# Storing an expert gate table in four 512 KB parts with 1 KB runs, and loading it back for eight expert blocks at a time

## The reference

```python
s1 = jnp.einsum('thd,kd->thk', q[:, :, 0], sub_k1)      # 8 heads, 128 keys on each side
s2 = jnp.einsum('thd,kd->thk', q[:, :, 1], sub_k2)
v1, i1 = lax.top_k(s1, 16); v2, i2 = lax.top_k(s2, 16)
cand = v1[..., :, None] + v2[..., None, :]
top, pos = lax.top_k(cand, 16)                          # 16 experts for each head and token
gate = jax.nn.softmax(top, axis=-1)
act = jax.nn.gelu(jnp.einsum('thkd,td->thk', u_tab[eidx], xb))
return jnp.einsum('thk,thkd->td', gate * act, v_tab[eidx])
```

## Time and profile before

| | us |
|---|---|
| median of 3 runs | 2424.49 |
| the runs | 2418.18, 2424.49, 2425.27 |
| the profiled execution, its own time | 2419.71 |
| its span (first to last instruction) | 2417.7 |
| TensorE busy | 2244.0 (93% of the span) |
| VectorE busy | 1726.0 (71%) |
| ScalarE busy | 909.4 (38%) |
| mean DMA rate over the span | 253 GB/s |

### The profile page before, as it was taken

How to read it: one execution, slowest core, us unless ns; L and a number is a source line. 1 busy time by engine, 2 the same in 40 slices (tenths; PEclk the granted TensorE clock), 3 DMA queues, 4 the chain that set the end, 5 groups by cost and what they waited for, 6 DMA issues and landing times.

```text
span 2417.7 us, 41224 instructions
## 1 busy us (share of the span) xinstructions
PE 2244.0 (93%) x16262; PEld 2080.3 (86%) x16262; DVE 1726.0 (71%) x3078; ACT 909.4 (38%) x1568; POOL 895.3 (37%) x1063
## 2 busy tenths in 40 slices
PE   6999987989899989899999899999998999999997
PEld 3877766877669988888999899999998999999997
DVE  4646586435735445568799887777876789999988
ACT  3333342220122111222344676666763333333333
POOL 3310310110304555336321044544444346565561
PEclk9988998998979999999999999999999999999999
DMA  5530740122818999858676489989999999999994
GB/s 154 178 94 18 241 130 20 56 84 71 280 72 255 303 293 308 249 164 300 196 246 210 156 281 350 334 316 348 324 342 378 388 376 397 405 404 403 403 405 184
DMA packets 328799, 611.62 MB, mean 253 GB/s; under 512 B 27712, under 2 KB 216144, under 8 KB 327584
## 3 DMA queue, kind: packets, MB, share of 16 engines
q0 software_dynamic: 90240, 316.05, 36.4%
q1 hardware_dynamic: 219936, 267.78, 33.1%
q10 hardware_dynamic: 18432, 25.17, 2.8%
HBM read 484.45 MB, written 124.45 MB: 252 GB/s over the span
## 4 chain that ended last, share of the span: by engine, by line
PE 57%; DVE 21%; DMA 15%; ACT 3%; issue 2%; POOL 2%; ACTq 0%; DVEq 0%; SPq 0%; POOLq 0%
PE PS L1197 56%; DMA RAW<-in_uT 8%; DMA u_rows<-arena 4%; DVE LO L2371 3%; DVE arena L1810 3%; DVE GU L2551 2%; DVE OH L2538 2%; POOL u_rows L605 2%; DVE arena L1849 1%; DVE arena L1819 1%; ACT HI L1060 1%; DVE arena L2066 1%; DVE arena L1816 1%; DVE BR L1849 0%; DVE rstd L1867 0%
## 5 line engine op out<-in xcount | busy, mean ns | idle before, releaser
L1060 ACT ACTIVATE HI<-RAW 128x1024 fp32r<-128x1024 f32 x256 | 272.6, 1065 | 456.6 <-PE PS L1197 155.5
L2371 DVE TENSOR_TENSOR LO<-RAW,HI 128x1024 fp32r<-128x1024 f32 x256 | 312.5, 1222 | 176.4 <-ACT HI L1060 175.6
L739 POOL DMA_INDIRECT GU<-u_rows,EIDX x160 | 255.6, 1598 | 408.3 <-DVE ACTG L2551 298.8
L1197 PE MATMUL PS<-XH,HI 128*128 128x384 f32 x1024 | 356.2, 348 | 29.1 <-DVE LO L2371 20.9
L1197 PE MATMUL PS<-HT,W 128*128 128x272 f32 (+1 forms) x1536 | 364.8, 398 | 18.0 <-DVE HT L1856 11.3
L1197 PEld LDWEIGHTS PS<-HT,W 128*128 128x128 f32 (+1 forms) x1536 | 284.7, 187 | 92.0 <-issue 27.3
L1197 PE MATMUL PS<-XL,HI 128*128 128x384 f32 x1024 | 347.1, 339 | 0.0
L1197 PE MATMUL PS<-XH,LO 128*128 128x384 f32 x1024 | 347.1, 339 | 0.0
L1197 PE MATMUL PS<-WH,HI 128*128 128x384 f32 x1024 | 343.4, 335 | 3.0 <-ACT AX L1101 3.0
L1197 PE MATMUL PS<-WL,HI 128*128 128x384 f32 x1024 | 343.2, 335 | 0.0
L1197 PE MATMUL PS<-WH,LO 128*128 128x384 f32 x1024 | 343.1, 335 | 0.0
(11 more groups left out here) (274 smaller groups left out, 3776.0 us busy)
## 6 DMA issues: line engine op xcount, KB each, us to landing
RAW<-in_uT SPq DMA_DIRECT2D x128, 512.0 KB, 5.9
RAW<-in_vT SPq DMA_DIRECT2D x128, 512.0 KB, 9.1
arena<-in_uT POOLq DMA_DIRECT2D x76, 512.0 KB, 5.4
W<-in_w_in SPq DMA_DIRECT2D x58, 512.0 KB, 5.3
u_rows<-arena POOLq DMA_DIRECT2D x216, 128.0 KB, 4.1
table_a<-AX ACTq DMA_DIRECT2D x128, 192.0 KB, 4.5
gate_table<-GST SPq DMA_DIRECT2D x12, 2048.0 KB, 17.1
AIN<-table_a SPq DMA_DIRECT2D x128, 192.0 KB, 10.4
```

The costliest lines, as they stand in the source:

```text
L739: pool.indirect_dma_start(out=GU[n % NGU][0:P], out_offset=None, in_=flat_u, in_offset=bass.IndirectOffsetOnAxis(ap=at, axis=0)).then_inc( ...
L1060: nc.scalar.activation(HI[:, s % NRING], RAW[:, s % NRING], ACT.Copy).then_inc(S("hi"), 1)
L1197: return nc.tensor.matmul(out, lhsT, rhs, start=first, stop=last)
L2371: dve.tensor_tensor(LO_[:, s % NRING], RAW[:, s % NRING], HI[:, s % NRING].bitcast(F32), ALU.subtract).then_inc(S("lo"), 1)
```

## The change

The gate table in HBM is laid out for groups of eight expert blocks (`EQT` = 8) in place of four, so the contiguous run of a store, for one expert row, is 8 x 32 gates, 1 KB, and was 512 B. Each group's store is cut into four parts (`GPARTS`), 512 KB each, of which each is issued behind another block load, and the first part stands two steps later than the whole store did. The parts of the last group all stand behind the last load of the first pass. `GQ` doubles in size, is loaded in two halves of 768 KB, and lies in the memory of `GST`, which is done with by then. At the start of the second pass both halves of the first buffer are loaded, 1.5 MB, before the second block load; before, it was 768 KB there and 768 KB behind the second block load.

```diff
-EQT = 4
+EQT = 8
+GPARTS = 4
...
-        GST = sb("GST", [P, 2, P, EB])
+        GST = sb("GST", [P, 2, P, EB], stack=part)
+        part.close()
         GQ = sb("GQ", [P, 2, NEB, EQT, EB])
+        sb("GST_rest", [P, 2 * P * EB - 2 * NEB * EQT * EB])
...
-            def store_gates(k):
-
-                sp.wait_ge(S("ge"), 8 * (k + 1))
-                sp.dma_start(gate_table[:, :, k * EQT * EB:(k + 1) * EQT * EB].rearrange("g p n -> p g n"),
-                             GST[:, k % 2].rearrange("p (g e) t -> p g (e t)", e=EQT)).then_inc(S(f"gw{k % 2}"), 16)
+            def store_gates(k, part):
+
+                if part == 0:
+                    sp.wait_ge(S("ge"), 8 * (k + 1))
+                g = slice(part * NQT // GPARTS, (part + 1) * NQT // GPARTS)
+                sp.dma_start(gate_table[g, :, k * EQT * EB:(k + 1) * EQT * EB].rearrange("g p n -> p g n"),
+                             GST[:, k % 2].rearrange("p (g e) t -> p g (e t)", e=EQT)[:, g]).then_inc(S(f"gw{k % 2}"), 16)
...
-            def load_gates(q):
+            def load_gates(q, half):
 
                 if q >= 2:
                     sp.wait_ge(S("gm"), EQT * (q - 1))
-                sp.dma_start(GQ[:, q % 2].rearrange("p a b c -> p (a b c)"), gate_table[q]).then_inc(S(f"lg{q % 2}"), 16)
-
-            stores = {copy_slot(8 * k + 7) + 4: k for k in range(NEB)}
-            assert len(stores) == NEB and max(stores) < NK
+                n = NEB * EQT * EB // 2
+                sp.dma_start(GQ[:, q % 2].rearrange("p a b c -> p (a b c)")[:, half * n:(half + 1) * n],
+                             gate_table[q][:, half * n:(half + 1) * n]).then_inc(S(f"lg{q % 2}"), 16)
+
+            stores = [(min(copy_slot(8 * k + 7) + 6 + i, NK - 1), k, i) for k in range(NEB) for i in range(GPARTS)]
             for s in range(NK):
                 load_raw(s)
-                if s in stores:
-                    store_gates(stores[s])
+                for at, k, i in stores:
+                    if at == s:
+                        store_gates(k, i)
...
             for e in range(3):
                 load_raw(NK + e)
                 load_act(e)
-                if e < 2:
-                    load_gates(e)
+                if e == 0:
+                    load_gates(0, 0)
+                    load_gates(0, 1)
             for e in range(3, NK):
                 load_act(e)
                 load_raw(NK + e)
-                if e % EQT == EQT - 2 and e // EQT + 1 >= 2 and e // EQT + 1 < NQT:
-                    load_gates(e // EQT + 1)
+                if e % EQT in (3, 5) and e // EQT + 1 < NQT:
+                    load_gates(e // EQT + 1, e % EQT // 5)
```

More of the change, by code:

```diff
@@ L546, in load_act @@
                 sp.dma_start(AIN[:, e % NAX], table_a[e]).then_inc(S(f"ain{e % NAX}"), 16)
-            def load_gates(q):
+            def load_gates(q, half):
                 if q >= 2:
                     sp.wait_ge(S("gm"), EQT * (q - 1))
-                sp.dma_start(GQ[:, q % 2].rearrange("p a b c -> p (a b c)"), gate_table[q]).then_inc(S(f"lg{q % 2}"), 16)
-            stores = {copy_slot(8 * k + 7) + 4: k for k in range(NEB)}
-            assert len(stores) == NEB and max(stores) < NK
+                n = NEB * EQT * EB // 2
+                sp.dma_start(GQ[:, q % 2].rearrange("p a b c -> p (a b c)")[:, half * n:(half + 1) * n],
+                             gate_table[q][:, half * n:(half + 1) * n]).then_inc(S(f"lg{q % 2}"), 16)
+            stores = [(min(copy_slot(8 * k + 7) + 6 + i, NK - 1), k, i) for k in range(NEB) for i in range(GPARTS)]
             for s in range(NK):
                 load_raw(s)
-                if s in stores:
-                    store_gates(stores[s])
+                for at, k, i in stores:
+                    if at == s:
+                        store_gates(k, i)
             for i in range(2):
-                sp.wait_ge(S(f"gw{i}"), 16 * ((NEB + 1 - i) // 2))
+                sp.wait_ge(S(f"gw{i}"), 16 * GPARTS * ((NEB + 1 - i) // 2))
             for e in range(3):
@@ L1145, in copy_unit @@
                 if u % 8 == 0 and k >= 2:
-                    act.wait_ge(S(f"gw{k % 2}"), 16 * (k // 2))
+                    act.wait_ge(S(f"gw{k % 2}"), 16 * GPARTS * (k // 2))
                 act.wait_ge(S("ohf"), u + 1)
@@ L2397, in weigh_act @@
                     q = e // EQT
-                    dve.wait_ge(S(f"lg{q % 2}"), 16 * (q // 2 + 1))
+                    dve.wait_ge(S(f"lg{q % 2}"), 32 * (q // 2 + 1))
                 x = AIN[:, e % NAX].rearrange("p (a t) -> p a t", t=EB)
```

## The result

The changed kernel takes 2387.86 us (median of 4 runs, 2378.22 to 2394.32), the kernel before 2421.79 us (median of 4, 2418.18 to 2425.27). The ratio of the runs is 0.9844, with a 95% interval from 0.981 to 0.9878: 30 to 46 us faster. The forecast was 2397, with 2386 to 2412 as its range; 0.9844 of 2421.79 is 2384 us, just under the range. The sign and the mechanism were right. The gain was sized more than a quarter too small: 22.5 us were forecast, and the medians differ by 33.9 us.

What follows compares the result with a forecast made beforehand. TensorE's products were taken to bound the kernel, and block loads where TensorE pauses. From the profiled execution, 2419.7 - 27.5 (pauses among the stores) + 5 (border) = 2397.2 us, said as 2397, range 2386 to 2412.

Steps and rivals of the forecast that it cites:

- The cause: First pass: ScalarE waits ten times, 105.8 us in all, for block loads late behind 2 MB stores; TensorE then pauses.
- The threshold: First pass: a block load costs TensorE nothing until its landing takes more than 8.9 + 7.7 = 16.6 us.
- The later first part: Stores of the first pass: issued two steps later, SyncE no longer waits 46.5 us for gates; worth nothing.
- second pass: Second pass: same bytes and pieces, landings stay under 16.6 us; no change, still 507 us.
- ScalarE's wait for a store before it reuses a half of `GST`: First pass: three steps, 15.6 us, cover a part's landing of 11.5 us, so ScalarE's queue isn't stopped.
- the first term: First pass, stores of groups 0 to 10 in four parts: gain 28.5 us, bounds 0 and 28.5, taken as 27.5.
- the border: Between the passes: last store behind load 127, pauses of 16.6 against 12.0 us; 4.6 us lost, taken as 5, range 0 to 10.
- Half is 0.75 us, 8 us over eleven stores. It is on no path: Stores in 1 KB runs: at most 1.5 us of DMA time saved per store, half taken; only pays for tighter packing.
- that the parts only spread the lateness: Rival, first pass: the fourth load lands at 18.4 us, 20 us idle in all; 2416, or 2406 with half; 17% in part.
- that DMA was the true limit: Rival: DMA engines, 0.95 busy, bound the kernel and pauses return elsewhere; no change, 2420 to 2425 us; 10%.
- The fixed time of each part: Rival: the queue pays some 2.1 us per part, loads land in 13.6 us, only the border pays; 2403 us; 6%.

Runs made afterwards that it cites:

- e2: Kernel before with only the four 512 KB parts between block loads, 512 B runs kept: 2393.25 us, ratio 0.9866 to the kernel before.
- e10: Kernel before with each whole 2 MB store in 512 B runs two block loads later: 2422.31 us in one run, against 2429.87 us.
- e5: Changed kernel with the last group's four parts together behind block load 125, ahead of loads 126 and 127: 2388.22 us in one run.
- e9: Changed kernel, last group's parts together behind load 125, and loads 128 and 129 with activations ahead of SyncE's wait for the stores: 2391.10 us, ratio 0.985.
- e11: Repeat of e5, timed in five rounds: 2389.95 us, ratio 0.9836 to the kernel before.
- e4: Changed kernel with two parts of 1 MB per group in place of four: 2397.39 us, ratio 0.9905 to the kernel before.
- e3: Changed kernel with each group's 2 MB in one store at the old place, 1 KB runs kept: 2408.90 us, ratio 0.993 to the kernel before.
- e1: The changed kernel again, unaltered, timed in five rounds: 2394.35 us against 2426.61 us for the kernel before, ratio 0.987.
- e8: Changed kernel with an extra unused 512 KB store behind each of block loads 52 to 123: 2457.75 us in one run.

## Why the prediction was right in kind and short in size

**The cause** held. A block load queued behind one store of 2 MB was late, once per group, and four parts with loads between them end it: e2 (parts alone) has the whole gain, e10 (place alone) none. Which of the two does it, the cut or the loads between, is not separated; at the last group the cut alone did (e5, e9, e11).

**The threshold** of 16.6 us held as a mean: in the changed kernel loads land in up to 13.5 us and TensorE never idles; in e4 up to 18.3 us, and it idles 1.5 us. For single stores it is not sharp. ScalarE's waits less TensorE's pauses, one store at a time in the kernel before and e3, give reserves from 6.6 to 9.9 us. In e3 the load behind the first store landed in 14.5 us, and TensorE paused 0.90 us and then 0.57 us:

```profile
DMA to landing us min/median/max: 14.5/14.5/14.5
...
1415.34 0.44 PE L1205 MATMUL PS<-XH,HI 128*128 128x384 f32 x1 [0.90 <-DVE LO L2379]
```

In the kernel before, the load behind the eleventh store landed in 18.4 us, and TensorE didn't pause at all. The prediction divided by ten stores, and there were eleven, but its pauses were also too small: 32.6 / 11 = 3.0 us against its 2.9, so the mean reserve stands.

**The later first part** cost nothing, as said, and neither did the **second pass** of the changed kernel (e3 and e4, with the same transfers there, lose 5.5 and 7.2 us in it). ScalarE's wait for a store before it reuses a half of `GST` cost nothing either, with less to spare than said: the margin was 15.6 us, a part was to land in at most 11.5 us, and in groups 0 to 10 parts took up to 15.5 us.

**The step that failed is the size of the first term**, "That is 28.5 us", of which 27.5 was taken, "for a pause or two that remain"; none remained. Measured: 32.6 us. I had added TensorE's idle time and the mean clock of the window, and both read low. A product is recorded as busy for twice the time after which the next one starts; a line group of the changed kernel's second pass (engine, operands, count, busy us, mean ns):

```profile
L1205 PE MATMUL PS<-WH,HI 128*128 128x384 f32 x972 | 324.6, 334 | 0.0
```

334 ns each, while 2916 products take 505 us, 173 ns each. So every pause is recorded some 0.16 us short, and the timeline of the kernel before has 13 pauses in that window: 2.1 us. And the clock of 0.99 is rounded: the trace has three stretches of 3.4 us at 1.2 GHz in place of 2.4, each behind the start of the products after a pause, which cost 5.1 us, not 4.2. Windows on the three (the clock stands behind POOL's count, as a share of 2.4 GHz):

```profile
1540.20:1543.60 3.40, 3.40 (x14) 3.40 (x13) 3.40 (x6) 3.40 (x9) 2.57 (x2) 0.51 0.53 177
1693.80:1697.20 3.40, 3.40 (x15) 3.40 (x14) 3.40 (x5) 3.40 (x8) 1.68 (x1) 0.51 0.85 277
1772.30:1775.70 3.40, 3.40 (x15) 3.40 (x14) 3.40 (x6) 3.40 (x8) 2.21 (x2) 0.51 0.71 262
```

Then 24.3 + 2.1 + 5.1 = 31.5 us; about 1 us stays unexplained. The plain way, the time of the same number of products at full speed, would have given it at once: 420.1 us against 387.7.

**The second size was the border**, "4.6 us lost", taken as 5. Measured: 1.2 us lost, 2.5 in e1. Its first half was close: the stores landed in 19.4 us (18.5 said), the gates 9.9 us later (9.0), the pause was 9.43 us (8.6). The second half was not: 1.91 us in step 128 where I had 5, and about 1.6 us of half speed where I had 3. The 5 was not worked out: it had only the order of ScalarE's work and the 3.04 us of the kernel before behind it. The half speed is less because the clock falls during the pause: of 10.2 us at half speed, TensorE has products in 3.2.

```profile
1826.20:1836.40 10.20, 3.20 (x10) 3.23 (x11) 5.51 (x9) 2.58 (x6) 1.68 (x1) 0.50 0.98 358
```

In a prediction such a stretch costs only what is left of it when the products start again.

Together the two terms are 9 us, the whole miss: 2419.7 - 32.6 + 1.2 = 2388.3 us, against a median of 2387.86. That the two agree within 0.5 us is luck, since single executions lie 16 us apart.

**"Half is 0.75 us, 8 us over eleven stores. It is on no path"** held for the parts (e2) and was the one place where I should have looked further: in whole stores it is on the path, and e3 shows 17 us for it in A, though a store's landing fell by no more than the 0.8 us that I had.

**The rivals**: that the parts only spread the lateness is refuted by the changed kernel's A, the same within 0.1 us in the eight runs that have four parts a group and no extra stores; that DMA was the true limit, by the window of 387.7 us with TensorE busy throughout, and by e8.

The fixed time of each part is not seen either: e5's four parts back to back land in less time than a whole store in the same place. The Trainium skill's wish for transfers of 1 MiB or more ("DMA: Bandwidth & Descriptors", section Bandwidth) would have spoken for e4's parts over the changed kernel's. By the trace they don't pay: e4's A is 3.8 us longer and its border 7.0 us. What counted is how late the load behind a part lands, up to 18.3 us in e4 and 13.5 us in the changed kernel, not the rate of the store. The fit of 2.0 us and 436 GB/s that the prediction took from this page of the Trainium skill stands in its section "Anatomy of one DMA" and is for transfers that GpSimd issues. The stores here are SyncE's, and no run here shows a fixed cost that adds up from part to part.

## What to carry to other kernels

When one in-order queue carries both loads with a deadline and bulk stores without one, cut the stores so that a piece and the load behind it land within the reserve of the engine that waits; moving the whole store by two steps did nothing. Measure that reserve as the wait of the first engine minus the idle time of the one that bounds the kernel, take it for a mean with 2 us to either side, and expect gains near the threshold not to add: shortening the store and splitting it cure the same pause. After an edit at the border of two stages, read the steady stage behind it too; here it took back what the border gave. Size a pause by the time of equal work at full speed elsewhere in the trace, not by recorded idle time and a rounded mean clock.

## What the runs showed of the hardware

- Four 512 KB stores in 1 KB runs issued back to back landed in 14.7 us (e5), where one store of the same 2 MB in the same place and the same runs took 21.8 us (e3). ScalarE then waited 7.8 us for the load behind the parts and 14.9 us for the load behind the one store. I expected no difference. The loads that followed and the gathers beside them were not held equal, so the reason stays open.
- The issue of a block load takes SyncE 0.33 us among the parts of the changed kernel. Behind a 2 MB store in 512 B runs it took 11.9 us (the `RAW` load at 1671.3 us of the kernel before), and SyncE issued nothing else in that time.
- Runs of 1 KB in place of 512 B lowered the DMA share by 0.02 at the same 365 GB/s (1.02 in e2, 0.99 and 1.00 in the changed kernel's two runs), and a whole store's landing by 0.8 us of 17.1.
- The first 1400 us took from 1386 to 1411 us in single executions of the thirteen runs, and the stages behind them repeated within 1.2 us for one and the same kernel. Nearly all of this spread is there when the first block load is issued (1108.5 to 1132.6 us); from that load to the end of the head it is 277 to 278 us in each run. The stage times tell apart what the medians can't.
- DMA moved 412 GB/s at a share of 1.04 when more was asked of it (e8), over the 397 GB/s of the second pass.
